# A two-layer decoder step on one core: the paged probabilities are transposed one step later, and first keys, stores and key eviction change their order

## The chip, the cores and the metric

The kernel runs on one core of one Trainium2 chip, as one launch for both layers. The time is device microseconds (us) of that core. The run before is the median of three executions. In the profile, PE is TensorE's matmul side and PEld its weight load, DVE is VectorE, ACT is ScalarE, POOL is GpSimd, and SP is the engine that issues most DMAs.

## What is computed

The reference is one inference step of a decoder with two layers, for a prompt group (1024 positions) and a sample group (8 sequences of 4 new positions, each with 4096 past positions in pages). Both groups share the weights. Cut to what matters:

```python
def trunk_layer(x, pos, attend, ...):
    h = rmsnorm(x, nm_pre)
    q_abs, q_pe, c_kv, k_pe, u, v = project(h, pos, ...)    # z = h @ w_in, split in five
    a_out = attend(q_abs, q_pe, c_kv, k_pe, w_uv)           # latent attention, 8 heads
    g_out = chunk_gating(u, v, w_s, b_s)                    # u * (tril(W_s) v + b)
    mix = jnp.einsum('bte,ed->btd', jnp.concatenate([a_out, g_out], axis=-1), w_out)
    x = x + rmsnorm(mix, nm_post)
    f = square(relu(rmsnorm(x, nf_pre) @ w_up)) @ w_down
    return x + rmsnorm(f, nf_post), c_kv, k_pe, v

def latent_attention(q_abs, q_pe, c_kv, k_pe, q_pos, k_pos, w_uv):
    s = (q_abs . c_kv + q_pe . k_pe) * ATTN_SCALE, masked to k_pos <= q_pos
    p = softmax(s)
    return (p . c_kv) @ w_uv
```

The prompt group attends to itself (causal). Each sample sequence attends to its 4096 paged positions and to its own new rows. The outputs are both groups' activations, the new latent and rotary keys of both, and the normalised v rows of the sample group (`o_vs`).

## The kernel before

All 1056 token columns (1024 + 32) lie side by side. The large projections (`dense`, L1647) split each weight tile and each activation into a high and a low part and run three passes. They fill TensorE from start to end in every stage but one, the attention, to which nearly all of the change belongs.

**The attention's loop.** It runs `for i in range(HALVES)`, 64 rounds in each layer, written out in program order on each engine. `JOBS` lists 32 jobs (u, j): head pair u, block j of 128 queries. A job has two halves (one head each), so round i handles half i of the prompt, in a pipeline: scores of half i+2 on TensorE (`scores`, L1830 and the mask L1833), their maximum on DVE (`maxima`, L1316), `exps` on ACT (L849), `normalise` on DVE (L1322, L1325), then `turn_p` on TensorE (L1842), which transposes the probabilities 128 columns at a time into a PSUM bank. The bank's first four blocks are copied out by ACT (`take_pt`, L862), and blocks 5 to 8 of a large job (j of 4 or more) form a second bank that DVE copies out (`take_pt`, L1339). `values(k)` (L1856) multiplies them with the values of job k, at the beginning of every even round. ACT and DVE evict its result (`take_o`, L856 and L1332).

**The paged work in it.** Four rounds make one step c (16 steps a layer, eight for each quad of four sequences). The phase is `ph = i % 4`. Phases 0 and 1 transpose four banks of latent keys fetched from the pages (`turn_keys`, L1877). Phase 2 ends with `step_scores` (L1888, L1890). DVE takes the maximum (`step_max`, L1382), ACT the exponential (`step_exp`, L884 and L886), and at the end of phase 3 `step_turn` (L1898) transposes these probabilities `pd`, which ACT copies out (`step_pt`, L891). `step_values` (L1909) uses them late in phase 0 of the next step. The new rows of a quad have a small step of their own in the quad's first step: `new_scores`, `new_exp` (L873), `new_turn` (L1928) at the end of phase 1, `new_pt`, and `new_values` (L1933) in phase 2.

**Jobs' sizes.** For u of 0 to 2 the jobs run 0, 7, 1, 6, 2, 5, 3, 4, so phases 0 and 1 hold a small job and phases 2 and 3 a large one. For u = 3 it is the other way round. Steps 0 to 11 belong to the first kind, steps 12 to 15 to the second.

**The ring.** All transposes go through PSUM banks 4 and 5 in turn. `ring_table` writes down the order in which the banks are filled and by whom each is emptied; `ring(key)` makes TensorE wait until the entry two places earlier has been emptied. `K_AT` names the rounds in which the keys of head pairs 2 and 3 are made (`keys_of`, L1778, one bank for each half of the positions) and copied out by ACT (half 0, L898 and L899) or DVE (half 1, L1358 and L1359).

**Ahead of the loop.** After the last query unit (L1733) and the last gating product (`mix`, L1758) TensorE makes the first keys and values, transposes the latent rows, and computes the first scores. SP moves the rotated queries (L507), stores `o_vs` (L510), spreads the rotary key (L513) into a place where the v rows lay, so that it waits for the store, and then issues the first gather of pages (L433, 16 DMAs).

The lines that set these waits on TensorE:

```python
def step_turn(c):
    pe.wait_ge(dexp.sem, at.value(dexp, c + c // CHUNKS + 2))
...
def turn_p(i, n):
    if n == 0:
        pe.wait_ge(p_new.sem, at.value(p_new, i + 1))
    bank = ring(("p", i, n))
```

Of the kernel before, what the change touches and what calls it, by code (L numbers as in the profile page):

```python
# [28 lines left out]
NS = DB * DT  # L29
TOK = SEQ + NS  # L30
NG, GW = 3, TOK // 3
NB = SEQ // P
# [41 lines left out]
K_AT = {19: (2, 0), 23: (2, 1), 35: (3, 0), 39: (3, 1)}  # L74


def ring_table():

    order = []
    for i in range(HALVES):  # L80
        ph, c = i % 4, i // 4
        big = JOBS[i // 2][1] >= 4
        order.append((("p", i, 0), "act"))
        if big:
            order.append((("p", i, 1), "dve"))
        if ph == 0:
            order += [(("d", c, 0), "act"), (("d", c, 1), "act")]
        if ph == 1:
            order += [(("d", c, 2), "dve"), (("d", c, 3), "act")]
            if c % CHUNKS == 0:  # L90
                order.append((("n", c // CHUNKS), "act"))
        if ph == 3:
            if i in K_AT:
                order.append((("k",) + K_AT[i], "act" if K_AT[i][1] == 0 else "dve"))
            order.append((("x", c), "act"))
# [57 lines left out]
def build(nc, xT, wst, gains, pre, wuq, wuk, wuv, wsp, bsp, cache_c, cache_k, pages, consts,  # L153
          yT, o_cp, o_kp, o_cs, o_ks, o_vs, x_spill):
    with ExitStack() as ctx:
# [257 lines left out]
        def _(sp):  # L413
# [7 lines left out]
            for l in range(DEPTH):  # L421
# [87 lines left out]
                sp.wait_ge(vt_free.sem, at.value(vt_free, NB + 1))  # L509
                sp.dma_start(o_vs[l], vn[0:NS, NB % 2, :]).then_inc(vs_out.sem, 16)  # L510
# [159 lines left out]
        def _(act):  # L670
# [98 lines left out]
            for l in range(DEPTH):  # L769
# [145 lines left out]
                exps(1)  # L915
                take_vals(6)
                take_cn(2)
                take_key(1, 0)
                take_key(1, 1)
                for i in range(HALVES):  # L920
# [5 lines left out]
                    take_pt(i)  # L926
                    if ph == 0:
                        take_keys(c, 0)
                        take_keys(c, 1)
                    if ph == 1:  # L930
                        take_keys(c, 3)
                        if c % CHUNKS == 0:
                            new_exp(c // CHUNKS)
                            if c == 0:
                                act.wait_ge(outs.sem, at.value(outs, 64))
                            new_pt(c // CHUNKS)
                    if ph == 3:
                        if i in K_AT and K_AT[i][1] == 0:
                            more_keys(K_AT[i][0])
                        step_exp(c)  # L940
                        step_pt(c)
# [100 lines left out]
        def _(dve):  # L1042
# [38 lines left out]
            for l in range(DEPTH):  # L1081
# [197 lines left out]
                for t in range(NB + 1):  # L1279
                    if t < UNITS_Q:  # L1280
                        take_q(t)
                    bias(t)
                    if t > 0:
# [3 lines left out]
                    if t == 6:  # L1287
                        low_w(0, at.whole(w_hi, 1))
# [121 lines left out]
                low_w(1, at.whole(w_hi, 2))  # L1410
# [4 lines left out]
                take_vals(3)  # L1415
                paged_ropes()
                take_vals(5)
                maxima(0)
                maxima(1)
                take_vals(7)  # L1420
                normalise(0)
                take_key(1, 0)
                take_key(1, 1)
                for i in range(HALVES):
# [17 lines left out]
                    if ph == 0:  # L1442
                        if c > 0:
                            step_out(c - 1)
                        if c % CHUNKS == 0:
                            new_max(c // CHUNKS)
                    if ph == 2:
                        if c % CHUNKS == 0:
                            new_out(c // CHUNKS)
                        step_max(c)  # L1450
# [822 lines left out]
```

## Time and profile before

| | |
|---|---|
| median of three executions | 2710.16 us (2709.4 to 2710.4) |
| the profiled execution: its time | 2707.71 us |
| the profiled execution: its span | 2705.9 us |
| attention of layer 0 (L1842's first to L1898's last) | 224.4 to 479.4 us |
| attention of layer 1 | from 1566.9 us |

The profiled execution lies 2.45 us under the median, and 1.81 us of its time lie outside the span. Layer 1 repeats layer 0 some 1342 us later. A row of the timeline gives the start in us, the busy time in us, engine, line, operation, what is written and read, the count of instructions merged, and in square brackets the idle time before it and what ended it. Busy times of consecutive matmuls overlap: four transposes of 128 columns are 0.66 us busy, but the next matmul starts 0.44 us after the first. So the moment at which TensorE could have gone on is taken as the end of the row before less 0.16 us, and a wait costs from there to the start of the waiting matmul.

### The profile page before, as it was taken

What the parts mean: (1) busy time and instruction counts of PE and PEld (TensorE: products, weight loads), DVE (VectorE), ACT (ScalarE), POOL (GpSimd) and SP (SyncE); (2) the same over time, 40 slices, a digit from 0 to 9 for tenths busy, and PEclk for the clock granted to TensorE, in tenths of its full rate; (3) what the DMA queues carried; (4) which work ended last, traced back from release to release, by engine and by line L of the source; (5) the groups of instructions that cost most, each with busy time, mean ns of one, the idle gap of its engine ahead of it and who ended that gap; (6) DMA issues with size and microseconds to landing.
All of it is one profiled execution on the core that took longest, in us unless ns stands there. A gap on an engine that the chain in (4) does not pass through costs nothing.

```text
span 2705.9 us, 42299 instructions
## 1 busy us (share of the span) xinstructions
PE 2611.9 (97%) x17128; PEld 2362.7 (87%) x17128; DVE 1133.2 (42%) x1626; ACT 658.6 (24%) x1111; POOL 778.9 (29%) x367
## 2 busy tenths in 40 slices
PE   8999999999999999999999999999999999999996
PEld 6985666979999999999879866669799999999995
DVE  5556666264222222221764566652732123222226
ACT  3125555141100110010241255551411000100111
POOL 2331000303433443333214300003033334433441
PEclk9999999999999999999999999999999999999998
DMA  6114232221111111111231243313211111111113
GB/s 218 47 36 127 81 83 68 112 88 44 43 47 47 47 42 44 47 47 47 104 111 40 56 119 82 85 54 118 80 47 47 47 47 42 43 47 47 47 41 134
DMA packets 91491, 185.96 MB, mean 69 GB/s; under 512 B 29664, under 2 KB 42144, under 8 KB 91360
## 3 DMA queue, kind: packets, MB, share of 16 engines
q1 hardware_dynamic: 88656, 175.75, 20.2%
q0 software_dynamic: 2560, 8.39, 1.1%
q8 instruction: 91, 1.49, 0.2%
q14 instruction: 40, 0.33, 0.0%
q10 hardware_dynamic: 144, 0.00, 0.0%
HBM read 157.77 MB, written 23.11 MB: 67 GB/s over the span
## 4 chain that ended last, share of the span: by engine, by line
issue 47%; PE 30%; POOLq 10%; DVE 7%; ACT 3%; DVEq 1%; POOL 1%; DMA 0%; SPq 0%; ACTq 0%
POOLq L604 9%; PE psum L1647 9%; PE psum L1830 3%; PE psum L1856 3%; PE psum L1677 3%; PE psum L1842 2%; PE psum L1632 2%; PE psum L1877 2%; PE psum L1733 1%; ACT z L849 1%; DVE sacc L1095 1%; DVE z L1142 1%; PE psum L1890 1%; POOL wl L605 1%; PE psum L1909 1%
## 5 line engine op out<-in xcount | busy, mean ns | idle before, releaser
L603 POOL TENSOR_TENSOR wh<-raw,ones 128x1024 fp32r<-128x1024 f32 x152 | 292.0, 1921 | 1286.3 <-PE psum L1647 1094.5
L1647 PE MATMUL psum<-hh,wh 128*128 128x352 f32 x2064 | 448.1, 325 | 3.0 <-issue 2.6
L1647 PE MATMUL psum<-hh,wl 128*128 128x352 f32 x2064 | 444.8, 323 | 0.0
L1647 PE MATMUL psum<-hl,wh 128*128 128x352 f32 x2064 | 444.3, 323 | 0.0
L605 POOL TENSOR_TENSOR wl<-raw,wh 128x1024 fp32r<-128x1024 f32 x152 | 419.5, 2760 | 22.0
L997 ACT ACTIVATE z<-z 128x1056 f32<-128x1056 f32 x64 | 69.7, 1089 | 1224.8 <-DVE stat L1504 1200.4
L1647 PEld LDWEIGHTS psum<-hh,wh 128*128 128x128 f32 x2064 | 351.5, 189 | 6.4 <-issue 5.1
L1647 PEld LDWEIGHTS psum<-hh,wl 128*128 128x128 f32 x2064 | 354.3, 188 | 0.0
L1647 PEld LDWEIGHTS psum<-hl,wh 128*128 128x128 f32 x2064 | 350.4, 188 | 0.0
L1500 DVE SCALAR_TENSOR_TENSOR z<-psum,rinv 128x1056 f32<-128x1056 f32 x64 | 80.5, 1257 | 552.6 <-PE psum L1647 542.8
L1520 DVE TENSOR_TENSOR z<-psum,z 128x1056 f32<-128x1056 f32 x104 | 130.8, 1257 | 394.6 <-PE psum L1647 341.7
L1647 PE MATMUL psum<-hidh,wh 128*128 128x352 f32 x1056 | 228.4, 324 | 0.0
L1647 PE MATMUL psum<-hidh,wl 128*128 128x352 f32 x1056 | 227.6, 323 | 0.0
L1647 PE MATMUL psum<-hidl,wh 128*128 128x352 f32 x1056 | 227.4, 323 | 0.0
L1647 PEld LDWEIGHTS psum<-hidh,wl 128*128 128x128 f32 x1056 | 181.4, 188 | 0.0
L1647 PEld LDWEIGHTS psum<-hidh,wh 128*128 128x128 f32 x1056 | 179.9, 189 | 0.0
L1647 PEld LDWEIGHTS psum<-hidl,wh 128*128 128x128 f32 x1056 | 179.3, 188 | 0.0
L626 POOL DMA_INDIRECT z<-cache_k,krows x32 | 30.8, 962 | 398.8 <-DVE cn L1352 394.6
L1493 DVE TENSOR_TENSOR hidl<-z,hidh 128x1056 fp32r<-128x1056 f32 x64 | 128.6, 2010 | 12.3 <-ACT hidh L999 11.7
L849 ACT ACTIVATE z<-psum,stat 128x128 f32<-128x128 f32 (+7 forms) x128 | 94.7, 740 | 70.9 <-DVE stat L1316 68.5
L1095 DVE TENSOR_TENSOR sacc<-sacc,t 128x1056 f32<-128x1056 f32 x45 | 70.5, 1567 | 78.8 <-ACT t L959 75.3
L1842 PEld LDWEIGHTS psum<-cst,z 128*128 128x128 f32 x576 | 63.8, 141 | 45.2 <-issue 37.0
(237 smaller groups left out, 3600.7 us busy)
## 6 DMA issues: line engine op xcount, KB each, us to landing
raw<-wst SPq DMA_DIRECT2D x160, 512.0 KB, 3.3
z<-cache_c SPq DMA_DIRECT2D x352, 64.0 KB, 1.8
x<-x_spill SPq DMA_DIRECT2D x4, 4224.0 KB, 14.2
raw<-cache_c SPq DMA_DIRECT2D x160, 64.0 KB
x_spill<-x SPq DMA_DIRECT2D x2, 4224.0 KB, 13.4
x_spill<-x SPq DMA_DIRECT2D x6, 1408.0 KB, 5.2
x<-xT SPq DMA_DIRECT2D x8, 528.0 KB, 8.2
yT<-x SPq DMA_DIRECT2D x6, 704.0 KB, 3.3
```

What stands on the lines that cost most here:

```text
L603: pool.tensor_tensor(wh[:, s, :], raw[:, s, :], ones[:, 0:1].to_broadcast([P, TW]), ALU.mult)
L604: pool.drain()
L605: pool.tensor_tensor(wl[:, s, :], raw[:, s, :], wh[:, s, :].bitcast(F32), ALU.subtract).then_inc(split.sem, 1)
L849: act.activation(probs[e][:, 0:(j + 1) * P], s_of(e, j), ACT.Exp, bias=stat[:, 32 + e:33 + e], accum_out=stat[:, 36 + e:37 + e]).then_inc( ...
L1095: ins = dve.tensor_tensor(sacc[:, :], sacc[:, :], tmp[sl][:, :], ALU.add)
L1493: dve.tensor_tensor(hidl[:, j, :], z[:, 10 + j % 2, :], hidh[:, j, :].bitcast(F32), ALU.subtract).then_inc(hid_l.sem, 1)
L1520: ins = dve.tensor_tensor(groups(z[:, m, :]), acc(m), groups(z[:, m, :]), ALU.add)
L1647: ins = pe.matmul(bank3(u, g), w[:, s, o:o + P], m[:, k, cols(g)], start=(k == 0 and n == 0), stop=(k == kk - 1 and n == 2))
L1677: ins = pe.matmul(bank, u_w[w], m[:, k, cols(g)], start=(first and n == 0), stop=(last and n == 2))
L1830: ins = pe.matmul(ps[2 * e + h][:, 0:w], qs[e][0:KQ, u, tok(j)], keys[0:KQ, 2 * (u % 2) + e, 512 * h:512 * h + w], start=True, stop=not last)
L1842: ins = pe.transpose(bank[:, (kb % 4) * P:(kb % 4 + 1) * P], probs[e][:, kb * P:(kb + 1) * P], ident)
L1856: ins = pe.matmul(ps[6][64 * e:64 * e + 64, 0:P], vals[:, kb, (2 * u + e) * VD:(2 * u + e) * VD + VD], pts[2 * e + kb // 4][:, kb % 4, :], ...
```

## The change

The order of work changes on four engines; no instruction's size or count does.

- `step_turn(c)` moves from the end of phase 3 to phase 0 of the next step (only the last step's stays). There `turn_p(i, 0)` comes first, then `values(k - 1)`, then `step_turn(c - 1)`. In phase 2 `values(k - 1)` still comes first. ACT's `step_pt` and DVE's `step_sum` follow into phase 0.
- `new_turn` moves from the end of phase 1 into phase 2 behind `turn_p(i, 0)`, and `new_values` behind `step_scores`.
- `K_AT` moves each key bank one round earlier, from phase 3 to phase 2, behind `step_scores`.
- `ring_table` follows: in phase 0 the paged probabilities ("x") stand between the two banks of `turn_p`.
- Ahead of the loop: the store `o_vs` is issued between the two groups of query DMAs; `bias(7)` on DVE comes before `take_q(7)`; two `low_w` of DVE come later; `keys_of(1, 0)` and `keys_of(1, 1)` come before `vals_of(6)`, and their copies before other work; two waits move from the loop's start to `new_scores`.

```diff
-K_AT = {19: (2, 0), 23: (2, 1), 35: (3, 0), 39: (3, 1)}
+K_AT = {18: (2, 0), 22: (2, 1), 34: (3, 0), 38: (3, 1)}
@@ ring_table
         order.append((("p", i, 0), "act"))
+        if ph == 0 and c > 0:
+            order.append((("x", c - 1), "act"))
+        if ph == 2 and c % CHUNKS == 0:
+            order.append((("n", c // CHUNKS), "act"))
         if big:
             order.append((("p", i, 1), "dve"))
...
@@ SP
+                    if a == 0:
+                        sp.wait_ge(vt_free.sem, at.value(vt_free, NB + 1))
+                        sp.dma_start(o_vs[l], vn[0:NS, NB % 2, :]).then_inc(vs_out.sem, 16)
@@ DVE, ahead of the loop
-                    if t < UNITS_Q:
+                    if t < UNITS_Q - 1:
                         take_q(t)
                     bias(t)
+                    if t == UNITS_Q - 1:
+                        take_q(t)
...
-                    if t == 6:
-                        low_w(0, at.whole(w_hi, 1))
@@ TensorE, ahead of the loop
-                vals_of(6)
...
                 keys_of(1, 0, key_bank(1, 0)[:, :]).then_inc(k_full.sem, 1)
                 pe.wait_ge(v_dve.sem, at.value(v_dve, 3))
                 keys_of(1, 1, key_bank(1, 1)[:, :]).then_inc(k_full.sem, 1)
+                vals_of(6)
+                vals_of(7)
@@ TensorE, the loop
-                    if i % 2 == 0 and k > 0:
+                    if ph == 2:
                         values(k - 1)
                     turn_p(i, 0)
+                    if ph == 0 and c > 0:
+                        values(k - 1)
+                        step_turn(c - 1)
+                    if ph == 2 and c % CHUNKS == 0:
+                        new_turn(c // CHUNKS)
                     if i + 2 < HALVES:
                         scores(i + 2, 0)
...
                     if ph == 2:
                         step_scores(c)
+                        if c % CHUNKS == 0:
+                            new_values(c // CHUNKS)
+                    if i in K_AT:
+                        u, h = K_AT[i]
+                        keys_of(u, h, ring(("k", u, h))).then_inc(t_full.sem, 1)
                     if ph == 3:
...
-                        step_turn(c)
```

Two places show how the rows move. The first is TensorE at the turn from step 0 to step 1 in layer 0, that is from phase 3 with job 7 to phase 0 with job 1. L1842 is `turn_p` (L1852 in the changed file), L1898 is `step_turn` (L1908 there), L1856 is `values` (L1866 there), L1830 `scores` (L1840 there). Before:

```order
L1842 MATMUL psum<-cst,z 128x128 [waits t_dve]
L1842 MATMUL psum<-cst,z 128x128 x3
L1898 MATMUL psum<-cst,z 128x128 [waits t_act,dexp]
L1898 MATMUL psum<-cst,z 128x128 x3
L1856 MATMUL psum<-t,scratch 64x128 [waits t_dve,o_new,t_act,do_free]
L1856 MATMUL psum<-t,scratch 64x128 x15
L1842 MATMUL psum<-cst,z 128x128 [waits t_dve,p_new]
L1842 MATMUL psum<-cst,z 128x128
L1830 MATMUL psum<-scratch,free_a 128x512 [waits exped]
```

In the changed kernel, at the same place:

```order
L1852 MATMUL psum<-cst,z 128x128 [waits t_dve]
L1852 MATMUL psum<-cst,z 128x128 x3
L1852 MATMUL psum<-cst,z 128x128 [waits t_act,p_new]
L1852 MATMUL psum<-cst,z 128x128
L1866 MATMUL psum<-t,scratch 64x128 [waits t_dve,o_new,t_act,do_free]
L1866 MATMUL psum<-t,scratch 64x128 x15
L1908 MATMUL psum<-cst,z 128x128 [waits t_dve,dexp]
L1908 MATMUL psum<-cst,z 128x128 x3
L1840 MATMUL psum<-scratch,free_a 128x512 [waits exped]
```

The wait for the normalised probabilities (`p_new`) now stands right behind the last transposes of phase 3, and the wait for the paged exponential (`dexp`) stands behind `values`.

The second place is TensorE in phase 2 of step 0, where the quad's new rows are handled. L1928 is `new_turn` (L1941 in the changed file), L1933 `new_values` (L1946 there), L1888 and L1890 `step_scores` (L1898 and L1900 there). Before:

```order
L1928 MATMUL psum<-cst,z 32x128 [waits t_dve,dexp]
L1856 MATMUL psum<-t,scratch 64x128 [waits o_new,do_free,t_act]
L1856 MATMUL psum<-t,scratch 64x128
L1842 MATMUL psum<-cst,z 128x128 [waits t_act,p_new]
L1842 MATMUL psum<-cst,z 128x128 x3
L1830 MATMUL psum<-scratch,free_a 128x256 [waits exped]
L1833 MATMUL psum<-trir,idr 128x128
L1842 MATMUL psum<-cst,z 128x128 [waits t_act]
L1842 MATMUL psum<-cst,z 128x128 x3
L1933 MATMUL psum<-cn 128x128 [waits o_new,t_act]
L1888 MATMUL psum<-z,sacc 32x512 [waits t_dve,t_act,rk_new,dexp]
```

In the changed kernel:

```order
L1866 MATMUL psum<-t,scratch 64x128
L1852 MATMUL psum<-cst,z 128x128 [waits t_dve,p_new]
L1852 MATMUL psum<-cst,z 128x128 x3
L1941 MATMUL psum<-cst,z 32x128 [waits t_act,dexp]
L1840 MATMUL psum<-scratch,free_a 128x256 [waits exped]
L1843 MATMUL psum<-trir,idr 128x128
L1852 MATMUL psum<-cst,z 128x128 [waits t_act]
L1852 MATMUL psum<-cst,z 128x128 x3
L1898 MATMUL psum<-z,sacc 32x512 [waits t_dve,t_act,rk_new,dexp]
L1898 MATMUL psum<-z,sacc 32x512 x3
L1900 MATMUL psum<-cn,sacc 128x512
L1946 MATMUL psum<-cn 128x128 [waits o_new,t_act]
```

The second bank of `turn_p` waits for ACT in both (`t_act`), but not for the same entry: before, two places back in the ring lay the small copy of `new_turn`; now it is the first bank of the same `turn_p`.

## Rows read from the trace of the kernel before

**Rows 1.** The page, part 1: busy time, share and instructions of each engine.
```profile
PE 2611.9 (97%) x17128; PEld 2362.7 (87%) x17128; DVE 1133.2 (42%) x1626; ACT 658.6 (24%) x1111; POOL 778.9 (29%) x367
```

**Rows 2.** Waits of PE, both layers: us in total, times, longest.
```profile
PE psum L1898 <- ACT z L886: 19.7, 22, 2.3
...
PE psum L1928 <- ACT z L873: 3.8, 4, 1.0
...
PE psum L1933 <- DVE hl L1332: 2.1, 2, 1.1
```

**Rows 3.** Timeline, turn from step 0 to step 1, layer 0.
```profile
238.19 0.60 PE L1842 MATMUL psum<-cst,z 128*128 128x128 f32 x4
238.82 0.69 DVE L1339 COPY t<-psum 128x512 f32<-128x512 f32 x1 [0.44 <-PE psum L1842]
239.43 0.66 PE L1898 MATMUL psum<-cst,z 128*128 128x128 f32 x4 [0.64 <-ACT z L886]
239.66 0.35 DVE L1325 TENSOR_SCALAR z<-z,stat 128x256 f32<-128x256 f32 x1
240.02 1.97 PE L1856 MATMUL psum<-t,scratch 128*64 128x128 f32 x32
...
397.79 0.38 PE L1842 MATMUL psum<-cst,z 128*128 128x128 f32 x2
398.78 0.49 DVE L1325 TENSOR_SCALAR z<-z,stat 128x512 f32<-128x512 f32 x1
```

**Rows 4.** Timeline, ends of steps 4 and 5, with key banks.
```profile
300.87 0.59 ACT L899 ACTIVATE scratch<-psum 64x512 f32<-64x512 f32 x1
302.50 0.66 PE L1898 MATMUL psum<-cst,z 128*128 128x128 f32 x4 [2.26 <-ACT z L886]
...
317.27 1.02 PE L1778 MATMUL psum<-z,sacc 128*128 128x512 f32 x2
318.17 0.63 PE L1898 MATMUL psum<-cst,z 128*128 128x128 f32 x4
318.18 0.42 DVE L1325 TENSOR_SCALAR z<-z,stat 128x384 f32<-128x384 f32 x1
```

**Rows 5.** Timeline, phase 2 of step 0, layer 0.
```profile
233.06 1.11 ACT L849 ACTIVATE z<-psum,stat 128x1024 f32<-128x1024 f32 x1 [0.79 <-DVE stat L1316]
233.20 0.60 PE L1842 MATMUL psum<-cst,z 128*128 128x128 f32 x4
234.33 0.60 ACT L862 ACTIVATE t<-psum 128x512 f32<-128x512 f32 x1
234.91 0.46 PE L1933 MATMUL psum<-cn 32*128 32x128 f32 x2 [1.11 <-DVE hl L1332]
```

**Rows 6.** Timeline, phase 0 of step 15 (u = 3).
```profile
463.87 0.60 ACT L862 ACTIVATE t<-psum 128x512 f32<-128x512 f32 x1
464.62 1.06 PE L1877 MATMUL psum<-cst,z 128*128 128x128 f32 x8 [0.71 <-ACT t L862]
```

**Rows 7.** Timeline, ahead of the loop; last row layer 1.
```profile
208.00 0.58 SPq L510 DMA_DIRECT2D o_vs<-scratch  x1
...
210.94 0.66 SPq L513 DMA_DIRECT2D scratch<-z  x1
...
217.67 0.46 PE L1830 MATMUL psum<-scratch,free_a 96*128 96x128 f32 x2 [0.90 <-issue]
...
224.36 0.30 PE L1842 MATMUL psum<-cst,z 128*128 128x128 f32 x1 [1.09 <-DVE scratch L1293]
...
224.93 0.14 PEld L1877 LDWEIGHTS psum<-cst,z 128*128 128x128 f32 x1 [0.24 <-DMA z<-cache_c]
...
1566.88 0.30 PE L1842 MATMUL psum<-cst,z 128*128 128x128 f32 x1 [1.09 <-DVE scratch L1293]
```

**Rows 8.** Windows of 1 us: PE, PEld, DVE, ACT, POOL busy, clock, DMA, GB/s.
```profile
206.00:207.00 1.00, 1.00 (x2) 0.34 (x1) 0.77 (x4) 0.02 (x1) 0.75 (x1) 0.50 0.33 76
...
1550.00:1551.00 1.00, 1.00 (x2) 0.34 (x1) 0.89 (x1) 0.00 (x0) 0.45 (x1) 0.50 1.11 241
```

More of the change, by code:

```diff
@@ L89, in ring_table @@
             order += [(("d", c, 2), "dve"), (("d", c, 3), "act")]
-            if c % CHUNKS == 0:
-                order.append((("n", c // CHUNKS), "act"))
-        if ph == 3:
+        if ph == 2:
             if i in K_AT:
                 order.append((("k",) + K_AT[i], "act" if K_AT[i][1] == 0 else "dve"))
-            order.append((("x", c), "act"))
+        if ph == 3:
+            if c == STEPS - 1:
+                order.append((("x", c), "act"))
             if c == CHUNKS:
@@ L1415, in _ @@
                 take_vals(3)
+                low_w(0, at.whole(w_hi, 1))
                 paged_ropes()
                 take_vals(5)
+                low_w(1, at.whole(w_hi, 2))
                 maxima(0)
                 maxima(1)
-                take_vals(7)
-                normalise(0)
                 take_key(1, 0)
                 take_key(1, 1)
+                normalise(0)
+                take_vals(7)
                 for i in range(HALVES):
@@ L1447, in _ @@
                     if ph == 2:
+                        step_max(c)
                         if c % CHUNKS == 0:
                             new_out(c // CHUNKS)
-                        step_max(c)
-                    if ph == 3:
-                        if i in K_AT and K_AT[i][1] == 1:
-                            more_keys(K_AT[i][0])
-                        step_sum(c)
+                    if i in K_AT and K_AT[i][1] == 1:
+                        more_keys(K_AT[i][0])
                 take_o(len(JOBS) - 1)
+                step_sum(STEPS - 1)
                 step_out(STEPS - 1)
@@ L1994, in _ @@
                         turn_keys(c, 2)
-                    if ph == 2:
-                        if c % CHUNKS == 0:
-                            new_values(c // CHUNKS)
                     if next_big:
@@ L2007, in _ @@
                         turn_keys(c, 3)
-                        if c % CHUNKS == 0:
-                            new_turn(c // CHUNKS)
                     if ph == 2:
                         step_scores(c)
+                        if c % CHUNKS == 0:
[3 more added lines that the diff above has]
+                        keys_of(u, h, ring(("k", u, h))).then_inc(t_full.sem, 1)
                     if ph == 3:
-                        if i in K_AT:
-                            u, h = K_AT[i]
-                            keys_of(u, h, ring(("k", u, h))).then_inc(t_full.sem, 1)
                         if c == STEPS - 1:
@@ L2022, in _ @@
                             out_part(0, (4, 5, 6, 7))
-                        step_turn(c)
+                            step_turn(c)
                         if c == CHUNKS:
```

41 lines of the change are left out of this document (21 added, 20 removed).

## The prediction

> **What bounds the kernel now.** I read the page's part 1 first: PE is busy 97% of the span [rows 1], so only what makes TensorE wait can matter, and every other engine has room. Second the waits of PE, by line. The largest entry is the wait of `step_turn` (L1898) for the paged exponential, 19.7 us in 22 waits over both layers; `new_turn` (L1928) waits 3.8 us and `new_values` (L1933) 2.1 us [rows 2]. These are the waits that the change goes for. An idle time leaves out the 0.16 us by which back-to-back matmuls overlap, so 22 waits cost 19.7 + 22 x 0.16 = 23.2 us; some of the other eight, too short to show as idle, bring it to 24.5 us, 12.2 a layer. Third the timeline at each of the 15 turns from one step to the next, because the question is what TensorE meets when `step_turn` is taken away there. The reader should look at DVE at that place, not at ACT.
>
> **Steps 0 to 10, the term that decides.** At the end of step 0 the last transposes of phase 3 start at 238.19, and TensorE could go on at 238.79 - 0.16 = 238.63. It waits for ACT until 239.43: 0.80 us lost [rows 3]. In the changed kernel the next matmul is the first transpose of the next half, and it needs that half normalised. DVE does this in its program order behind the copy of the very bank that TensorE has just filled: the copy starts at 238.82, the multiplication starts at 239.66 and ends at 240.01 [rows 3]. With 0.05 us for the signal TensorE starts at 240.06, 1.43 us after it was free. Before, that wait was covered by `step_turn` and 1.9 us of `values` (L1856 at 240.02) [rows 3]; now both stand behind it and cover nothing. DVE's part starts from TensorE's own transposes, so it can't come earlier relative to them, and the diff leaves DVE's order in phase 3 alone up to the multiplication.
>
> Worked out alike, the wait is 1.43 at steps 0, 4 and 8, between 1.31 and 1.38 at steps 1, 2, 5, 6, 9 and 10, and 0.96 and 0.98 at steps 3 and 7, where DVE's copy is one block; the last of the eleven is step 10, where TensorE is free at 398.17 - 0.16 = 398.01 and DVE ends at 399.27, so 1.31 [rows 3]. Sum 14.3 us a layer. What goes away in the same eleven steps is 0.80, 0.70, 0.60, 1.31, 2.50, 0.04, 0.59, 1.32, 2.43, 0.04 and 0.59, together 10.9. Steps 4 and 8 lose most now, because ACT copies out a key bank first, two copies of 0.59 (the second at 300.87), and `step_turn` starts at 302.50 only [rows 4]. Steps 5 and 9 lose nothing now, since the key bank (L1778, 1.02 us busy) covers the exponential [rows 4]; with the keys gone to phase 2, TensorE is free at 317.27 and DVE ends at 318.60 [rows 4], so 1.38 us appear from nothing. Net **+3.4 us a layer**. The later `step_turn` finds its exponential ready: it was there for 239.43 [rows 3], and TensorE now comes for it at 240.06 + 0.22 + 1.9 = 242.2.
>
> **The key banks in phase 2.** `keys_of` follows `step_scores` and costs TensorE the same 0.86 us as before. But in the ring the second bank of phase 3 must now wait until the key bank is emptied: two copies of 0.59 on ACT or 0.67 on DVE, 1.2 to 1.4 us from the end of the matmul, while TensorE fills only some 0.7 to 0.9 us with a `turn_p` and a `scores`. That is 0.5 us at three of the four places and 0.15 at the fourth, where an old wait of 0.4 is covered. **+1.6 us.**
>
> **The new rows (steps 0 and 8).** `new_turn` now has its exponential, but it pushes `turn_p`'s second bank behind its own first bank. At step 0 ACT starts an exponential of 1024 columns at 233.06 and copies that first bank out from 234.33 to 234.93 [rows 5]. Before, TensorE made the second bank at 233.20 and then waited at `new_values` until 234.91 [rows 5]. After, TensorE is free at about 232.35 and waits until 235.0. The two old waits of 1.1 and 1.25 us turn into one of 2.65 and two small ones: +0.5 us. At step 8 the same sum gives 0. **+0.5 us.**
>
> **Steps 11 to 14 (phase 0 large).** Here the wait for DVE shrinks: 0.96 at step 11 and 0.08 to 0.16 at the others, since no DVE copy stands in phase 3. But phase 0 now has the ring order first bank, paged bank, second bank. At step 15 ACT's copy of the first bank runs from 463.87 to 464.47, and TensorE's latent keys start at 464.62 [rows 6]. Afterwards the second bank waits for that copy, and the keys wait for the paged bank's copy behind it on ACT, 0.6 us more: keys at 465.07. Such sums give +0.4, -0.2, +0.4 and +0.45. **+1.0 us.**
>
> Inside the loop: 3.4 + 1.6 + 0.5 + 1.0 = 6.5, rounded up from the unrounded terms to 6.6 us a layer, **13.2 us** in both.
>
> **Ahead of the loop.** `mix(8)` waits for `bias(7)`, which no longer stands behind `take_q(7)`: 0.45 us earlier. SP stores `o_vs` at 208.00, behind the second group of query moves, and the spread of the rotary key follows only at 210.94, when the store has landed; the first scores start at 217.67, 6.7 us after it [rows 7]. With the store issued some 8 us earlier, the spread can go at about 208.7, and the scores' wait of 1.1 us goes. The last wait before the loop, 1.09 us idle for a key copy [rows 7], ends behind `vals_of(6)`, `vals_of(7)` and the latent transposes, which now lie between; some 0.3 us stay. That makes 2.7 us, less 0.1, because the pages' first gather was only just in time already (the weight load at 224.93 waited 0.24 us for it) [rows 7]: 2.6 us. In layer 1 the same last wait is there, at 1566.88 [rows 7], but the scores don't wait for the key spread, since TensorE comes later: its clock stood at 0.50 in both layers [rows 8], but for 3.4 us in layer 0 and for 6.8 us in layer 1. So layer 1 gains 1.6 us. Together **-4.2 us**; the bounds are 0 (if DVE's delayed `low_w` hold up the key copies) and -7.
>
> **Sum.** 13.2 - 4.2 = +9.0 us on the profiled execution's own 2707.7, that is 2716.7. That execution lies 2.45 us under the median of the three runs, which is what is predicted: 2710.2 + 9.0 = **2719.2 us**.
>
> **A price that the trace does not show here.** TensorE's clock stood at 0.50 of full speed (1.2 GHz) around 206 us, shortly before the loop, and at the same place in layer 1 [rows 8]; a wait of 2.26 us before 302.50 [rows 4] did not bring it down. The new wait of 2.65 us in step 0 is longer than any in today's loop. A fall there would cost, by the 6.8 us at half clock in layer 1, up to 3.4 us a layer, and by layer 0's 3.4 us at least 1.7. The Trainium skill ("TensorE: Matmul & The Clock Gate", section on HAM oscillation) says that idle gaps between bursts of matmuls let the array fall back to half rate, and that this is paid again at each such gap. By that rule the moved wait costs more than its length; no row shows it at a wait inside the loop. I leave it out of the sum and keep it as a rival.
>
> **The rivals.**
> - *The wait moves to the normalised probabilities*, as summed: 2719, with 2716 to 2722 as its own range (the ahead-of-loop gain off by 2 either way, the ring's waits by 1). Chance 0.60.
> - *The same, and the clock falls in the new wait of step 0* in one or both layers: 1.7 to 6.8 us more, 2721 to 2726. For it speaks that the clock did fall ahead of the loop [rows 8], against it that the loop's waits of up to 2.3 us [rows 2] brought no fall. Chance 0.14.
> - *The ring costs nothing*: ACT and DVE empty key and first banks in time after all, because TensorE arrives later everywhere. Then only the decided term stays: 2 x 3.4 - 4.2 = +2.6, 2712.8, up to 2715. Chance 0.18.
> - *The change does what its order aims at*: it ends faster if the normalised half is there when TensorE is free. Then the 12.2 + 2.2 + 1.5 = 16 us a layer that the old waits cost are gone, less some 7 us of ring waits: -18 - 4 = -22 us, 2688. It decides at one place, the start of DVE's multiplication against the end of the last transposes of phase 3: it would have to come 1.4 us sooner than in rows 3. DVE's order speaks against it. Chance 0.08.
>
> **How the numbers follow.** A measurement of this kernel can tell about 0.2%, 5.4 us, from no change. The first two cases lie above 2715.6: slower 0.74. The third is within: 0.18. The fourth is faster: 0.08. The range of 2711 to 2725 leaves out the fourth, the end of the second and a little below the third, about 0.15 in all.
>
> **What would show it.** In the profile after, the wait of L1908 for ACT should be gone from the list of PE's waits, and L1852 (`turn_p`) should wait for DVE's L1334 in about 22 places at 1.2 us idle each at the longest, some 25 us in all. L1852 should also wait for ACT's L867, longest about 2.5 us, at step 0 of each layer. Before the loop, the first L1840 should start near 216 and the first L1852 near 221.8. The prediction is wrong if L1852's wait for DVE is under 10 us in sum, or if the attention of layer 0, measured from the first `turn_p` on, is not 5 us longer or more.

## The result and the profile after

The changed kernel takes **2727.66 us** (median of six runs, 2722.60 to 2731.68), the kernel before 2709.78 in the same comparison (2706.97 to 2710.67). The ratio is 1.0067, with a 95% interval of 1.0054 to 1.0081: 17.9 us slower. The profiled execution took 2724.72 us with a span of 2722.9, against 2707.71 and 2705.9: 17.0 us more.

The page of the changed kernel, its first line and the line of PE in part 1, which answers to [rows 1]:

```profile
span 2722.9 us, 42299 instructions
PE 2619.4 (96%) x17128; PEld 2367.0 (87%) x17128; DVE 1131.9 (42%) x1626; ACT 655.1 (24%) x1111; POOL 778.6 (29%) x367
```

PE is 7.5 us longer *busy* with the same 17128 instructions. Waits that show as idle time can't do that. A lower clock can, and so can waits too short to show.

The waits of PE, both layers, for [rows 2]. L1852 is `turn_p`, L1887 `turn_keys`, L2037 the transposition of quad 0's output (entry "f" of the ring):

```profile
PE psum L1852 <- DVE z L1334: 25.2, 24, 1.3
...
PE psum L1852 <- ACT t L867: 11.0, 8, 3.0
...
PE psum L1852 <- ACT scratch L904: 1.4, 4, 0.4
PE psum L1852 <- DVE scratch L1368: 1.4, 4, 0.3
PE psum L1887 <- ACT t L867: 1.0, 4, 0.3
PE psum L2037 <- ACT t L867: 1.0, 2, 0.5
```

`step_turn`, `new_turn` and `new_values` wait no more. In their place `turn_p` waits for the normalised half (first row), for the first bank's copy (second), and for the key banks (next two). The timeline at the turn from step 0 to step 1, for [rows 3]:

```profile
238.50 0.60 PE L1852 MATMUL psum<-cst,z 128*128 128x128 f32 x4
239.14 0.69 DVE L1348 COPY t<-psum 128x512 f32<-128x512 f32 x1 [0.75 <-PE psum L1852]
239.98 0.35 DVE L1334 TENSOR_SCALAR z<-z,stat 128x256 f32<-128x256 f32 x1
240.39 0.44 PE L1852 MATMUL psum<-cst,z 128*128 128x128 f32 x2 [1.28 <-DVE z L1334]
240.75 1.97 PE L1866 MATMUL psum<-t,scratch 128*64 128x128 f32 x32
242.65 0.55 PE L1908 MATMUL psum<-cst,z 128*128 128x128 f32 x3
```

TensorE is free at 238.94 and starts at 240.39: 1.45 us, where the prediction had 1.43. Both covers, `values` (L1866) and `step_turn` (L1908), stand behind the wait. At the ends of steps 4 and 5, for [rows 4], the same wait is 1.29 and 1.22 us idle.

Phase 2 of step 0, for [rows 5], and the windows of the three stretches at half clock in layer 0's loop (columns as in [rows 8]; the clock is the third figure from the end). Such a stretch is called a fall from here on:

```profile
229.51 0.28 PE L1941 MATMUL psum<-cst,z 128*32 128x128 f32 x1
229.63 0.60 PE L1840 MATMUL psum<-scratch,free_a 96*128 96x256 f32 x2
229.88 0.41 PE L1843 MATMUL psum<-trir,idr 128*128 128x128 f32 x1
232.87 0.96 PE L1852 MATMUL psum<-cst,z 128*128 128x128 f32 x4 [2.58 <-ACT t L867]
233.76 1.94 PE L1898 MATMUL psum<-z,sacc 128*32 128x512 f32 x8
```

```profile
232.80:236.20 3.40, 3.33 (x13) 1.26 (x14) 1.85 (x4) 0.52 (x3) 0.00 (x0) 0.54 0.44 145
...
321.60:325.00 3.40, 3.40 (x31) 2.99 (x30) 0.01 (x1) 0.80 (x3) 0.00 (x0) 0.53 0.05 19
372.80:376.20 3.40, 3.40 (x34) 3.07 (x34) 0.00 (x0) 0.44 (x2) 0.00 (x0) 0.53 0.00 0
```

Behind the 2.58 us of idle time four transposes take 0.96 instead of 0.66, and eight score matmuls 1.94 instead of 1.07. These stretches are at 1.2 GHz, but for the first 0.2 to 0.3 us of each window. Layer 0's loop had none before, layer 1's had one and now has two, the new one at its step 0. There the clock is at 0.50 from 1584.8 on, while TensorE waits until 1585.32, so this fall began in the wait and not behind it.

Both loops whole, from the first `turn_p` to the last `step_turn`, first before, then after (columns: length, PE busy, PEld, DVE, ACT, POOL, clock):

```profile
224.40:479.70 255.30, 240.13 (x2140) 161.62 (x2141) 158.32 (x375) 142.26 (x341) 12.29 (x13) 1.00 0.29 83
1566.90:1823.60 256.70, 241.54 (x2137) 162.83 (x2138) 158.31 (x375) 142.24 (x341) 12.28 (x13) 0.99 0.30 81
```

```profile
222.20:490.20 268.00, 246.96 (x2138) 165.13 (x2138) 158.50 (x373) 141.31 (x343) 12.31 (x13) 0.98 0.27 79
1574.20:1840.70 266.50, 245.01 (x2138) 163.60 (x2138) 158.51 (x373) 141.11 (x343) 12.31 (x13) 0.99 0.28 80
```

The first of these windows ends 0.3 us behind the start of the last `step_turn` (479.41), the others at it. From start to start layer 0's loop is 12.9 us longer, and layer 1's 9.8. Idle time (length less PE busy) grew from 15.2 to 21.0 and from 15.2 to 21.5. The rest, 7.0 and 3.5 us, is longer busy time: the clock, and waits under some 0.16 us that don't show as idle. The part ahead of the loop of layer 0, for [rows 7] (L515 the store, L518 the key's spread, L1840 the first scores):

```profile
199.57 0.58 SPq L515 DMA_DIRECT2D o_vs<-scratch  x1
...
208.80 0.65 SPq L518 DMA_DIRECT2D scratch<-z  x1
...
216.94 0.39 PE L1840 MATMUL psum<-scratch,free_a 96*128 96x128 f32 x2
...
222.24 0.30 PE L1852 MATMUL psum<-cst,z 128*128 128x128 f32 x1
```

The waits ahead of L1840 and L1852 are gone. The changed kernel reaches its first `turn_p` of layer 0 2.1 us earlier (222.24 for 224.36), although its first matmul of all started 1.1 us later (7.90 for 6.82, a wait for the first DMA of `x` that lies between 6.0 and 7.9 us in the fourteen traces, whatever the kernel). Counted from that matmul the gain is 3.2 us. From the last `step_turn` of layer 0 to the first `turn_p` of layer 1 it takes 3.4 us less (1084.0 for 1087.5). 12.9 + 9.8 - 2.1 - 3.4 = 17.2, against 17.0 in the spans; behind the loops 0.1 less is left.

### The profile page after: what moved, and what is told of

The parts are those of the page before. It is cut to its first block, busy times and chain, and to the rows that moved or that the text cites. A ratio compares the mean times of both kernels' runs of the same rounds, so it can differ in the third digit from the quotient of the medians.

```text
span 2722.9 us, 42299 instructions
## 1 busy us (share of the span) xinstructions
PE 2619.4 (96%) x17128; PEld 2367.0 (87%) x17128; DVE 1131.9 (42%) x1626; ACT 655.1 (24%) x1111; POOL 778.6 (29%) x367
## 4 chain that ended last, share of the span: by engine, by line
issue 47%; PE 34%; POOLq 10%; DVE 6%; ACT 2%; DVEq 1%; POOL 1%; DMA 1%; SPq 0%; ACTq 0%
POOLq L609 9%; PE psum L1657 9%; PE psum L1840 4%; PE psum L1687 3%; PE psum L1866 3%; PE psum L1852 3%; PE psum L1887 2%; PE psum L1642 2%; PE psum L1743 2%; PE psum L1900 1%; PE psum L1898 1%; PE psum L1919 1%; DVE sacc L1104 1%; POOL wl L610 1%; DVE z L1151 1%
## 5 line engine op out<-in xcount | busy, mean ns | idle before, releaser
L1852 PE MATMUL psum<-cst,z 128*128 128x128 f32 x576 | 101.5, 285 | 39.2 <-DVE z L1334 25.2
L1852 PEld LDWEIGHTS psum<-cst,z 128*128 128x128 f32 x576 | 64.2, 142 | 83.7 <-DVE z L1334 34.7
## 6 DMA issues: line engine op xcount, KB each, us to landing
x_spill<-x SPq DMA_DIRECT2D x2, 4224.0 KB, 12.9
```

What stands on the lines that cost most here:

```text
L1852: ins = pe.transpose(bank[:, (kb % 4) * P:(kb % 4 + 1) * P], probs[e][:, kb * P:(kb + 1) * P], ident)
```

## The experiments

My theory after the result: the moved transposition uncovers `turn_p`'s wait (the largest part), the new waits add falls of TensorE's clock, and the part ahead of the loop gains. Rivals: that the new rows or the key banks cost most, that the falls have nothing to do with idle time, and that the part ahead of the loop only shifts waits. All times are medians of four to eleven runs, beside the kernel before on the same chip, at 2709.43, 2709.01 and 2708.18 us in the three sets; the intervals are of the ratio to it. The changed kernel was measured only in the first comparison, beside 2709.78, so a difference to its 2727.66 is off by up to 1.6 us from set to set. Falls are counted in one profiled execution of each kernel.

**Only the part ahead of the loop** (the kernel before, with the diff's parts on SP, on DVE ahead of the loop, and of the first keys).

> Only the part ahead of the loop is changed (store, bias and query order on DVE, first keys before the values, waits moved to the new scores); the attention's loop keeps the order of before. My theory, that this part gains and the loop loses: 4 to 6 us under before, about 2704 to 2706, with no new fall of TensorE's clock inside the loop. Rival 1, that this part gains nothing of its own and only shifts waits into the first step: within 1 us of before. Rival 2, that a part of the loss is here: over before by 2 us or more.

2705.33 us, 0.9989 (0.9980 to 0.9998): 4.1 us faster. Its list of waits inside the loop is that of before, but for one wait of 0.9 us for the pages' first gather, which TensorE now reaches too early, and its only fall in a loop stands where the kernel before had its own. This part gains, and the loop loses all the more.

**The paged transposition back at the end of phase 3.**

```diff
-                    if ph == 2:
+                    if i % 2 == 0 and k > 0:
                         values(k - 1)
                     turn_p(i, 0)
-                    if ph == 0 and c > 0:
-                        values(k - 1)
-                        step_turn(c - 1)
...
                             out_part(0, (4, 5, 6, 7))
-                            step_turn(c)
+                        step_turn(c)
```

> The changed kernel with the paged probabilities transposed at the end of phase 3 again (and values ahead of the first transposition in every even round, the bank's place in the ring, the copy and the sum with it); new rows, key banks and the part ahead of the loop stay changed. My theory, that the moved transposition uncovers the wait for the normalised probabilities, which then also brings most of the clock's falls: 2707 to 2714, the list of PE's waits has the probabilities' transposition waiting for DVE's normalising under 2 us in sum, and the fall of the clock, if one is left in the loop, stands at step 0. Rival, that the new rows' wait at step 0 or the key banks in phase 2 cost most: 2720 or more.

2711.21 us, 1.0008 (0.9999 to 1.0017): of the 17.9 us 16 are gone by this move alone. The waits of its PE (L1846 is `turn_p`, L1902 `step_turn`):

```profile
PE psum L1902 <- ACT z L888: 15.0, 21, 1.3
...
PE psum L1846 <- ACT t L864: 7.8, 4, 3.2
```

The wait for DVE's normalising is off the list. The 2.58 us at step 0 are still there, and from about then on the clock stood at half for 10.2 us in layer 0:

```profile
230.95 1.11 PE L1846 MATMUL psum<-cst,z 128*128 128x128 f32 x4 [2.58 <-ACT t L864]
231.99 1.94 PE L1892 MATMUL psum<-z,sacc 128*32 128x512 f32 x8
233.86 2.08 PE L1894 MATMUL psum<-cn,sacc 128*128 128x512 f32 x2
235.87 0.79 PE L1940 MATMUL psum<-cn 32*128 32x128 f32 x2
236.59 1.11 PE L1846 MATMUL psum<-cst,z 128*128 128x128 f32 x4
```

Layer 1 has three falls of 3.4 us, one at step 0 and one at the end of each of steps 4 and 8, where TensorE waits 0.35 us behind a key bank and then 1.27 us at `step_turn`. In all the clock is at half for 20.5 us in the two loops of this execution (which lies 3.5 us over the median), for 17.1 in the changed kernel's. So the falls did not go with the wait for DVE here, as I had expected. This execution is 10.0 us shorter than the changed kernel's with no less time at half clock, and that much of the 16 us belongs to the waits. The rest may be falls that the medians have and these two executions don't: the mean clock over the runs is 0.988 in the middle here, and 0.986 to 0.987 in the changed kernel.

**Only the new rows back.**

```diff
-                    if ph == 2 and c % CHUNKS == 0:
-                        new_turn(c // CHUNKS)
...
                     if ph == 1:
                         turn_keys(c, 2)
+                    if ph == 2:
+                        if c % CHUNKS == 0:
+                            new_values(c // CHUNKS)
...
                         turn_keys(c, 3)
+                        if c % CHUNKS == 0:
+                            new_turn(c // CHUNKS)
```

> The changed kernel with only the new rows put back (their transposition at the end of phase 1, their values early in phase 2). My theory, in which step 0 costs 0.5 us a layer by its wait and one fall of the clock of about 2.4 us in both layers: 3 to 6 us under the changed kernel, 2722 to 2725, and no wait over 1.5 us at step 0. Rival, that the falls of the clock come from the sum of idle time and not from this one wait: they appear elsewhere, and the time stays within 1.5 us of the changed kernel's 2727.7.

2720.93 us, 1.0049 (1.0035 to 1.0062): 6.7 us under the changed kernel (6.4 with each beside its own kernel before), a little more than expected. At step 0 the longest wait is 1.1 us in layer 0 and 1.7 in layer 1, and neither layer has a fall there; but the profiled execution has two falls elsewhere in layer 0's loop (at 301.4 and 369.6) and one in layer 1's. So my theory and its rival each hold a part: the fall at step 0 belongs to that wait, and others come about among the short waits. The places of these others are few. In this kernel, the changed one and the one with the transposition back, all eight stand at the end of step 4, 5 or 8, where a key bank makes TensorE wait for 0.34 to 0.36 us and one or two more waits follow within 2 us (1.22 to 1.29, or 0.51 and 0.47). None stands behind a wait of 1.2 to 1.3 us that comes alone.

**The values first.** The values of the last job stand ahead of the first transposition in phase 0 too, and wait for the second bank only at their fifth block.

```diff
-                    if ph == 2:
+                    if i % 2 == 0 and k > 0:
                         values(k - 1)
                     turn_p(i, 0)
                     if ph == 0 and c > 0:
-                        values(k - 1)
                         step_turn(c - 1)
@@ values
-                        if j >= 4:
-                            evicted(RING_AT["p", 2 * k + e, 1])
...
+                        if kb == 4:
+                            for e in range(2):
+                                evicted(RING_AT["p", 2 * k + e, 1])
```

> The changed kernel, but in phase 0 the values of the last job stand ahead of the first transposition, as before the change, and wait for the second bank only at their fifth block; the paged transposition stays behind the probabilities' one. My theory: the values' 1.2 to 1.9 us cover the wait for the normalised half, whose 1.3 us at 22 places are gone, and the paged exponential stays covered too; without the falls that followed those waits 2688 to 2698. Rival, that the values now wait as long for the copies of the banks as the probabilities did for DVE: 2715 or more, with the waits at the values' line.

2695.36 us, 0.9951 (0.9938 to 0.9965): 32 us under the changed kernel and 14 under the one before. The same turn as above, with no wait left in it (L1867 the values, L1909 `step_turn`):

```profile
237.36 0.60 PE L1852 MATMUL psum<-cst,z 128*128 128x128 f32 x4
237.89 2.04 PE L1867 MATMUL psum<-t,scratch 128*64 128x128 f32 x32
239.86 0.44 PE L1852 MATMUL psum<-cst,z 128*128 128x128 f32 x2
240.13 0.60 PE L1909 MATMUL psum<-cst,z 128*128 128x128 f32 x4
```

In the loops only the fall at step 0 is left, in both layers. This kernel differs from the changed one in two things, the place of the values and the later wait for the second bank; no run has one without the other. Over three kernels with that wait of step 0 (the changed one, the transposition back, the values first), all six profiled layers have a fall there.

**The waits filled, too long.** Before asking what a fall costs, I had to fill the waits without shortening them.

```diff
+                    for _ in range({4: 24, 36: 9}.get(i, 0)):
+                        pe.matmul(ps[2 * e + h][:, 0:w], qs[e][0:KQ, u, tok(j)],
+                                  keys[0:KQ, 2 * (u % 2) + e, 512 * h:512 * h + w], start=True, stop=True)
...
+                    if ph == 0 and 0 < c < 12:
+                        pe.wait_ge(o_new.sem, at.value(o_new))
+                        pe.wait_ge(do_free.sem, at.value(do_free))
+                        for _ in range(8 if c % 4 == 0 else 12):
+                            pe.matmul(ps[6][:, 0:P], ident, ident, start=True, stop=True)
                     turn_p(i, 0)
```

> The changed kernel, with TensorE's waits filled by matmuls whose results are overwritten: ahead of each first transposition of phase 0 in steps 1 to 11 it makes 12 matmuls of 128 columns (8 where DVE's last copy is one block), about as long as the wait of 1.3 us (1.0 us), and ahead of the first scores of phase 2 at steps 0 and 8 it repeats that scores matmul 24 and 9 times. The waits stay as long as they were, and are only no longer idle. My theory, that the waits cost their length and the falls of the clock behind idle TensorE cost some 9 us more, which the prediction's sum left out: 2716 to 2721, and no stretch at half clock inside the two loops beyond those of before. Rival, that the falls have nothing to do with idle time: 2726 to 2732, with as many falls.

2765.41 us, 1.0211 (1.0197 to 1.0225): a miss in time. A filling matmul took twice what I had read from transposes, since each is two rows of the trace:

```profile
229.43 10.53 PE L1841 MATMUL psum<-scratch,free_a 96*128 96x256 f32 x48
```

24 repetitions are 48 rows and 10.5 us, 0.44 each, where the wait was 2.7. But neither loop of this profile has a fall.

> The run with the values first, with the same repeated scores (24 at step 0, 9 at step 8) and nothing else. There the two loops had one fall of the clock each, at step 0. My theory: both falls are gone and with them 3 to 4.5 us, 2691 to 2692.5. Rival, that what the new rows' wait costs is its length: within 1.5 us of 2695.4.

2712.07 us, 1.0008 (0.9999 to 1.0017), a miss by the same mis-sizing. The fill is 33 x 0.44 = 14.5 us a layer where the waits were 2.7 and 1.2, so 10.6 a layer and 21.2 in all are the fill's own; less these it is 2690.9, which is 4.5 under the run without fill. Both falls are gone. The loops of the two traces say less: they are 18.3 us longer than without fill, 2.9 under the fill's 21.2. As a time this stays worked out, not measured.

**The waits filled to their length** (`{4: 6, 36: 3}` and `range(4 if c % 4 == 0 else 6)`).

> The first filled kernel again, with the fill cut to the waits' length: in it a 128-column matmul turned out to take two passes of 0.11 us and a repeated scores matmul 0.44 us, so 6 matmuls (4 where DVE's last copy is one block) now stand ahead of the first transpositions of phase 0 in steps 1 to 11, and the scores matmul is repeated 6 times at step 0 and 3 times at step 8. Else the changed kernel. My theory, that the falls of the clock follow idle TensorE and cost what the prediction's sum left out: 2716 to 2722, with no fall in the loop's steps 0 to 11 (the fill itself may overshoot the waits by up to 0.1 us a place, 4 us in all, within this range). Rival, that the falls have nothing to do with the idle time: 2727 or more.

2719.77 us, 1.0041 (1.0027 to 1.0054): 7.9 us under the changed kernel (6.3 with each beside its own kernel before) with some 140 matmul rows *more* in each loop (2281 for 2138). These are the loops:

```profile
220.40:485.20 264.80, 258.50 (x2281) 179.44 (x2281) 158.44 (x373) 141.10 (x343) 12.29 (x13) 1.00 0.28 81
1570.50:1834.80 264.30, 258.30 (x2281) 179.52 (x2281) 158.45 (x373) 141.00 (x343) 12.22 (x13) 1.00 0.28 81
```

In these loops the clock is 1.00 throughout. Phase 2 of step 0 there, with the same rows as above behind a filled wait:

```profile
231.94 0.66 PE L1855 MATMUL psum<-cst,z 128*128 128x128 f32 x4
232.52 1.07 PE L1901 MATMUL psum<-z,sacc 128*32 128x512 f32 x8
...
235.98 0.60 PE L1855 MATMUL psum<-cst,z 128*128 128x128 f32 x4
```

The four transposes take 0.66 us for 0.96, the eight score matmuls 1.07 for 1.94, and the five runs lie within 1.7 us of each other (2718.55 to 2720.29) where the changed kernel's six lie within 9.1. The rival, that the falls have nothing to do with idle time, is out: nothing differs but that TensorE works in the waits. Whether it matters that the filling is matmuls and not transposes was not tested.

Step by step the two traces show that the waits kept their length, and what a fall costs. From `step_scores` of one step to that of the next the filled kernel takes as long as the changed one, within 0.02 us, at 24 of the 30 places. It is 1.61 and 1.62 us shorter at two of the changed kernel's falls (step 5 of layer 0, step 4 of layer 1) and 1.29 and 0.87 at the two of step 0, a part of which lies ahead of `step_scores`. At step 8 the fill was too long by 0.7 us in each layer: 0.70 more in layer 1, and 0.88 less in layer 0, where another fall stood. The changed kernel alone shows the same price, since its layers differ at step 5 (L1898 is `step_scores`; first layer 0 with the fall, then layer 1 without):

```profile
314.97 1.07 PE L1898 MATMUL psum<-z,sacc 128*32 128x512 f32 x8
...
334.06 1.06 PE L1898 MATMUL psum<-z,sacc 128*32 128x512 f32 x8
...
1668.77 1.07 PE L1898 MATMUL psum<-z,sacc 128*32 128x512 f32 x8
...
1686.24 1.07 PE L1898 MATMUL psum<-z,sacc 128*32 128x512 f32 x8
```

That is 19.09 us against 17.47: 1.6 us for a fall of 3.4.

**The new rows back as well as the values first.**

> The run with the values first, with the new rows put back as before the change (transposed at the end of phase 1, multiplied early in phase 2). My theory: 1 us for the waits and some 4 us for the two falls of the clock at step 0, so 2689 to 2692, with no fall in either loop. Rival, that the paged exponential or the old new_values wait of 1.7 us brings a fall of its own: 2694 or more.

2690.40 us, 0.9931 (0.9918 to 0.9945), as expected in time. But there is one fall left in each loop, at step 15 in layer 0 and, behind `new_values`' wait of 1.57 us, at step 0 in layer 1. I had expected none.

**The key banks back too.**

> As the run before, with the key banks in phase 3 too, so that of the loop's changes only the paged transposition behind the first transposition of the next phase 0 is left, with the values ahead of both. The prediction put the key banks in phase 2 at 1.6 us a layer; by that this is 3.2 us under the run before, 2686 to 2689. Rival, that in phase 3 they now make the values or the transposition wait, since the second bank is copied later: as fast as the run before or slower.

2689.38 us, 0.9923 (0.9909 to 0.9937). The two medians are 1.0 us apart, less than they can tell, so by time this is open. In the traces, with one fall in each loop of both kernels, the loops are 3.0 and 1.8 us shorter (248.1 for 251.1, 248.8 for 250.6); the prediction had put 1.6 a layer. No run puts only the key banks back in the changed kernel, where falls stand behind their waits, so what they cost there through the clock is open.

**The new rows' transposition behind the values.**

```diff
                         values(k - 1)
+                    if ph == 2 and c % CHUNKS == 0:
+                        new_turn(c // CHUNKS)
                     turn_p(i, 0)
...
                         step_scores(c)
+                        if c % CHUNKS == 0:
+                            new_values(c // CHUNKS)
```

> The last run (values first, new rows and key banks as before the change) with the new rows' transposition behind the values of phase 2 instead of ahead of them, and new_values behind step_scores, so that the 0.44 us of the values and the 3 us of scores cover their waits of 1.0 and 1.6 us. My theory: about 2 us of waits at step 0 and 1 at step 8 go in each layer, less what the ring gives back, 2681 to 2686. Rival, that the second bank's transposition then waits for ACT as long (as in the changed kernel at step 0): 2688 or more.

**2683.82 us**, 0.9911 (0.9898 to 0.9925): 24.4 us faster than the kernel before on that chip, and 43.8 under the changed kernel. Its loops have no fall and 6.7 and 6.2 us of idle time, for 15.2 before:

```profile
219.90:466.30 246.40, 239.66 (x2138) 161.19 (x2139) 157.62 (x373) 140.97 (x343) 12.31 (x13) 1.00 0.30 87
1550.10:1795.70 245.60, 239.36 (x2138) 161.21 (x2138) 157.73 (x373) 140.88 (x343) 12.31 (x13) 1.00 0.30 87
```

**In steps 12 to 15 the paged transposition behind the second bank.**

> The run before (new rows behind the values), and in steps 12 to 15, where phase 0 holds a large job, the paged transposition behind the second bank instead of between the two, so that the second bank no longer waits for the first one's copy. Expected from the waits of 1.3 us there: 1 to 3 us less than the run before. Rival, that the latent keys' banks take over the wait: no difference within 1 us.

2683.89 us, 0.9911 (0.9896 to 0.9926): no gain. `turn_p`'s wait for the copy (3.9 us in 4 waits in the run before) is gone, and `step_turn`, which needs the same copy for its bank, waits instead:

```profile
PE psum L1909 <- ACT t L868: 5.6, 8, 1.4
```

**Only the store ahead of the loop.**

> The kernel before with only the store of the v rows issued between the two groups of query moves. The prediction gave this 1.1 us in layer 0, where the first scores waited for the key's spread, and nothing in layer 1: 2708 to 2709 against 2709.4. Rival, that most of the 4 us ahead of the loop come from the store: 2706 or less.

2707.99 us, 0.9994 (0.9985 to 1.0003), against 2708.18: the interval takes in no change and the 1.1 us that I expected. Nor does it rule out the rival, since it reaches down to 2704.1. The trace speaks for the small figure: `scores` no longer wait, and the first `turn_p` of layer 0 comes 1.3 us earlier than in the kernel before, counted from the first matmul of each.

## Why the prediction was off

The direction and the mechanism were right, and so was the place of most of the loss; the time (2719.2, up to 2725) was too low by 8.5 us, or by 8.0 on the profiled executions (17.0 us more, where 9.0 were predicted). By its own signs of being wrong the mechanism holds: `turn_p` waits 25.2 us for DVE, not under 10, and layer 0's loop is 12.9 us longer, not under 5. By its own terms, on the profiled executions:

- **The sum for `turn_p`.** 24 waits of 25.2 us in all, longest 1.3, where about 22, 25 and 1.2 were predicted; 1.45 us at step 0 for 1.43. DVE's order decides, as said. Putting the transposition back took away 16 of the 17.9 us, some 10 of them by waits alone.
- **The new rows at step 0.** 2.65 us predicted, 2.74 measured in layer 0 (229.88 + 0.41 - 0.16 to 232.87). In layer 1 the wait shows 3.0 us of idle time: some 0.5 more than I gave it.
- **The loops without the clock.** A fall costs 1.6 us, as measured above, and 1.3 at step 0 of layer 1, where it began in the wait (1585.32 to 1590.69 is 5.37 us, against 4.04 for the same rows in the kernel filled to length, 231.94 to 235.98). With three falls in layer 0, and the new one in layer 1 (the one at its step 4 stood there before), that leaves 12.9 - 4.8 = 8.1 and 9.8 - 1.3 = 8.5 us a layer, where the sum had 6.6. Rows show where most of the 1.5 and 1.9 lie. A wait I had not seen, of the "f" transposition (L2037), is 0.51 idle and 0.16 more a layer. The key banks' four waits (1.4 + 1.4 + 8 x 0.16 = 4.1 us in both layers) came to 0.4 a layer more than predicted. From step 14 to step 15 a layer loses 0.94 us for the 0.45 of the prediction, since the second bank waits longer for the first one's copy than I had reckoned:

```profile
474.37 0.66 PE L1852 MATMUL psum<-cst,z 128*128 128x128 f32 x4 [1.17 <-ACT t L867]
```

- **Ahead of the loops.** -4.2 predicted. In the traces it is -5.5 with the first matmul's 1.1 us of chance, and -6.6 without them; 1.6 to 1.7 of the 3.4 in layer 1 is one fall shorter by 3.4 us, which leaves some 5 for the change. The experiment alone gave -4.1.
- **The step that failed: "A price that the trace does not show here."** I left the clock out of the sum and gave it 0.14 as a rival. The four falls that the changed kernel's loops have more than before cost 3 x 1.6 + 1.3 = 6.1 us of the 8.0. The median execution probably has more of them than the profiled one: the six runs go from 2722.60 us at a mean clock of 0.990 to 2731.68 at 0.985, and the profiled one had 0.988. That rival's own place, step 0 in both layers, was right, and its range of 2721 to 2726 came near; it missed the falls among the short waits. The Trainium skill ("TensorE: Matmul & The Clock Gate", section on a second HAM failure mode) says that frequent short idle times between groups of matmuls are enough for the clock to go up and down. The trace agrees: the falls at 321.6 and 372.8 stand behind waits of 0.34 and 1.22 us, and of 0.35, 0.51 and 0.47 us. It also shows that such waits need not bring one: behind 0.35 and 1.29 us at step 4 the clock fell in layer 1 and stayed up in layer 0. How many falls an execution gets could not be told from the waits alone.
- **Why I left it out.** I wrote that a wait of 2.26 us before 302.50 "did not bring it down", and took it for all of today's loop. It was one layer's. In layer 1 of the kernel before the same wait was followed by half clock; I had not read that row:

```profile
1644.99 0.66 PE L1898 MATMUL psum<-cst,z 128*128 128x128 f32 x4 [2.26 <-ACT z L886]
1645.58 3.56 PE L1856 MATMUL psum<-t,scratch 128*64 128x128 f32 x32
```

The 32 matmuls take 3.56 us there and 1.97 behind the same wait in layer 0 (303.08). The evidence against the rival was one case of two.

The sum, mended: 8.1 + 8.5 for the loops, 6.1 for the falls, -5.5 ahead, 17.2. This only sorts what the traces measured and forecasts nothing. It holds for the profiled execution; the medians lie 17.9 apart, or 17.5 with the median before that the prediction started from.

One slip in the part ahead of the prediction changes nothing: four transposes of 0.60 us busy are followed after 0.44, and four of 0.66 (first behind a wait) after 0.49 to 0.50. The overlap of 0.16 holds for both.

## What to carry to other kernels

Before a covering piece of work is moved away from a wait, ask what else waits at that place: here `step_turn` and `values` hid DVE's normalising, and the change moved both behind it. The covering work should not need the same late copy. With the values first again and their wait split at the fifth block, 17.9 us of loss became a gain of 14; the split's own share was not measured. Where a tuned loop's waits grow, price TensorE's clock too, and look at every layer's repetition of a wait before saying that the clock stays up: two layers of one execution, equal within 0.02 us elsewhere, differ by 1.6 us where one has a fall.

## What the runs showed of the hardware

- A fall of TensorE's clock came in or behind the idle time of 2.6 to 3.2 us at step 0 in six profiled layers of six. It lasted 3.4 us in five and 10.2 us in one, although TensorE was busy behind the wait. A fall of 3.4 us cost 1.6 us where TensorE worked through all of it. Behind the 2.26 us at step 4 it came in four layers of six (the kernel before, and the two kernels with its loop). Single waits of 1.2 to 1.3 us brought none, while eight falls stood behind two or three waits in a row of 0.34 to 1.29 us. With the waits at step 0 filled by matmuls there was no fall in six layers.
- A filled wait can gain: some 280 extra rows of matmuls in its two loops made the kernel 6.3 to 7.9 us faster.
- A transposition of 128 columns of f32 is one row of 0.11 us; a matmul of 128 columns of f32 by f32 is two such rows, 0.22 us. So transposes don't price a matmul.
